# The recurrence's steps stand between the projections of its gate and of attention's queries and keys, which use two banks there in place of four

## The reference

```
z = xn @ w_in
qa = rmsnorm(qa.reshape(B, T, A_HEADS, HEAD_DIM), q_gain)
ka = rmsnorm(ka.reshape(B, T, A_HEADS, HEAD_DIM), k_gain)
...
attn = einsum('bnthk,bnshk->bnhts', q_dec, k_in) * mask
o_intra = einsum('bnhts,bnshv->bnthv', attn, v)
u = einsum('bnshk,bnshv->bnhkv', k_out, v)
def step(s, inp):
    d, uu = inp
    return d[..., None] * s + uu, s
...
o = o_intra + o_inter            # o_inter from q_dec and the state before the block
ob = rmsnorm(ob, out_gain) * silu(gb)
z = concatenate([oa, ob]); out = z @ w_out
```

## Time and profile before

| | us |
|---|---|
| median of 3 runs (1215.68 to 1221.85) | 1216.68 |
| the profiled execution, its own time | 1219.2 |
| its span in the profile | 1217.5 |
| end of the last projection unit | 227.0 |
| first score maximum of attention | 276.4 |
| mean granted clock of TensorE | 0.921 |

### The profile page before, as it was taken

The page is one execution under the profiler, slowest core; times in us unless marked ns, Lnnn a source line. Parts: engine busy times, 40 slices in busy tenths (PEclk is TensorE's granted clock), DMA queues, the critical chain, the costliest instruction groups (busy, mean ns, idle before and its releaser), DMA issues.

```text
span 1217.5 us, 20227 instructions
## 1 busy us (share of the span) xinstructions
PE 1027.6 (84%) x8691; PEld 802.2 (66%) x8691; DVE 435.5 (36%) x935; ACT 282.5 (23%) x543; POOL 181.0 (15%) x146
## 2 busy tenths in 40 slices
PE   5998999777999899977777299999998999778771
PEld 4988999654599755543444199999997555444440
DVE  5324584357734711100110574565446111011104
ACT  4244322115721211211111422222211112111110
POOL 4344331002000012111111000000000122111010
PEclk9999999856989999988888689999999999898886
DMA  6322321401084779999998713323578699999956
GB/s 215 84 78 72 102 83 38 112 11 53 13 306 178 279 271 418 416 417 416 416 415 309 233 52 88 105 80 129 208 128 348 257 416 416 416 417 416 416 239 229
DMA packets 114862, 282.83 MB, mean 232 GB/s; under 512 B 22954, under 2 KB 70102, under 8 KB 98356
## 3 DMA queue, kind: packets, MB, share of 16 engines
q1 hardware_dynamic: 105044, 263.66, 58.5%
q0 software_dynamic: 9728, 17.85, 4.0%
HBM read 270.57 MB, written 27.02 MB: 244 GB/s over the span
## 4 chain that ended last, share of the span: by engine, by line
PE 57%; DMA 24%; DVE 9%; SPq 4%; ACT 2%; issue 2%; POOL 1%; DVEq 0%; POOLq 0%; ACTq 0%
DMA w<-in_w_dram 19%; PE banks L1010 12%; PE banks L938 11%; PE banks L660 8%; PE banks L878 8%; PE banks L949 4%; PE banks L659 3%; SPq L389 3%; DMA wab<-in_w_in_ab_dram 2%; DVE XF L1289 2%; DMA yab<-y_rows 1%; POOL wab_lo L563 1%; PE banks L837 1%; PE banks L821 1%; PE banks L635 1%
## 5 line engine op out<-in xcount | busy, mean ns | idle before, releaser
L938 PE MATMUL banks<-w,xgT 128*64 128x256 f32 x2048 | 258.4, 412 | 73.4 <-DMA w<-in_w_dram 72.3
L938 PEld LDWEIGHTS banks<-w,xgT 128*64 128x64 f32 x2048 | 161.0, 149 | 179.2 <-DMA w<-in_w_dram 75.6
L1655 DVE TENSOR_TENSOR hh<-banks,sg 128x128 f32<-128x128 f32 x64 | 18.7, 292 | 412.6 <-ACT sg L1220 412.6
L575 POOL DMA_INDIRECT y_rows<-ys,yidx x64 | 63.7, 995 | 386.9 <-ACT ys L1228 385.6
L949 PE MATMUL banks<-w,hT 128*64 128x512 f32 x512 | 116.9, 598 | 0.0
L1010 PE MATMUL banks<-xc_hi,wc_hi 128*128 128x272 f32 x384 | 111.8, 291 | 2.1 <-DVE xc_lo L1302 2.1
L1010 PE MATMUL banks<-xc_hi,wc_lo 128*128 128x272 f32 x384 | 112.3, 292 | 0.0
L1010 PE MATMUL banks<-xc_lo,wc_hi 128*128 128x272 f32 x384 | 111.5, 290 | 0.0
L571 POOL DMA_INDIRECT xr<-x_rows,gidx x32 | 33.5, 1045 | 417.5 <-DVE yidx L1640 399.3
L660 PE MATMUL banks<-wab_hi,xc_hi 128*128 128x256 f32 (+1 forms) x320 | 91.4, 286 | 0.7 <-POOL wab_lo L563 0.7
L660 PE MATMUL banks<-wab_hi,xp_lo 128*128 128x256 f32 (+1 forms) x320 | 90.4, 283 | 0.0
(11 more groups left out here) (284 smaller groups left out, 1803.7 us busy)
## 6 DMA issues: line engine op xcount, KB each, us to landing
w<-in_w_dram SPq DMA_DIRECT2D x192, 1024.0 KB, 22.8
wab<-in_w_in_ab_dram SPq DMA_DIRECT2D x13, 1024.0 KB, 5.1
wc<-in_w_in_c_dram SPq DMA_DIRECT2D x24, 512.0 KB, 6.2
yab<-y_rows SPq DMA_DIRECT2D x16, 512.0 KB, 7.0
wo<-in_w_out_ab_dram SPq DMA_DIRECT2D x4, 1024.0 KB, 5.4
x_rows<-XF SPq DMA_DIRECT2D x8, 512.0 KB, 9.6
wo<-in_w_out_c_dram SPq DMA_DIRECT2D x4, 1024.0 KB, 5.6
H<-in_x_prompt_dram SPq DMA_DIRECT2D x4, 512.0 KB, 8.3
```

The source lines that it names most:

```text
L575: pool.indirect_dma_start(y_dram[l][:, :], bass.IndirectOffsetOnAxis(ap=index.bitcast(U32), axis=0), ys[i][:, :], None, bounds_check=4 * T ...
L938: last = pe.matmul(bank[hb][64 * f:64 * f + 64, 0:2 * P].rearrange("p (w j) -> p w j", w=2), xgT[i][:, k, 64 * ab:64 * ab + 64], w13[s][:, ...
```

## The change

Units 26 to 48 (output gate, queries, the first half of the keys) now alternate between banks 0 and 1 alone, so a unit waits for the one two earlier. Banks 2 to 7 go to the recurrence, whose steps stand between these units: keys and products of chunk c after unit 27+c, the updates of chunk 0 after unit 32, then for each chunk a pattern of three units: output of c and updates of c+1 behind unit 34+3c, `hgrn_T` of c behind unit 36+3c. DVE's chain of states is cut in halves, one each behind the reading of units 34+3c and 35+3c. Unit 49, the first on four banks again, waits for the whole recurrence (`st_ok` and `zB_ok` at 5). The values' units keep only `rows_T`, and attention follows the last of them. Several tiles move in SBUF (states, `kr`, `am`, `zB`); no arithmetic changes.

```
+SHARED = range(FIRST[6], FIRST[11])
+UNIT_BANK = [u % 2 if u in SHARED else u % 4 for u in range(UNIT_END[-1])]
...
-            return len([u for u in range(unit + 1) if u % 4 == b])
+            return len([u for u in range(unit + 1) if UNIT_BANK[u] == b])
...
             def unit(n, a):
                 u_ = FIRST[n] + a
+                b = UNIT_BANK[u_]
                 if u_ >= 4:
-                    pe.wait_ge(z_free[u_ % 4], u_ // 4)
+                    pe.wait_ge(z_free[b], freed(u_, b) - 1)
+                if u_ == SHARED.stop:
+                    pe.wait_ge(st_ok, NC)
+                    pe.wait_ge(zB_ok, NC)
...
             def hgrn_T(c):
                 n = ROWS[c]
                 pe.wait_ge(zt_ok, c + 1)
-                pe.wait_ge(a_ok, NC)
-                if c >= 2:
-                    pe.wait_ge(zB_ok, c - 1)
+                pe.wait_ge(st_ok, min(c + 2, NC))
...
             for n in range(1, 14):
                 pe.wait_ge(w_lo, n + 1)
                 for a in range(UNITS[n]):
                     unit(n, a)
+                    beside = FIRST[n] + a - SHARED.start
+                    if 1 <= beside <= NC:
+                        hgrn_keys(beside - 1)
+                        hgrn_products(beside - 1)
+                    if beside == 6:
+                        hgrn_updates(0)
+                    if 8 <= beside <= 20 and beside % 3 == 2:
+                        c = (beside - 8) // 3
+                        hgrn_out(c)
+                        if c + 1 < NC:
+                            hgrn_updates(c + 1)
+                    if 10 <= beside <= 22 and beside % 3 == 1:
+                        hgrn_T((beside - 10) // 3)
                     if n >= 12:
                         rows_T(NC * (n - 12) + a)
-                        i = NC * (n - 12) + a
-                        (hgrn_products if i % 2 else hgrn_keys)(i // 2)
-            hgrn_updates(0)
-            for c in range(NC):
-                if c + 1 < NC:
-                    hgrn_updates(c + 1)
-                if c > 0:
-                    hgrn_T(c - 1)
-                hgrn_out(c)
...
+            def hgrn_chain(c, half):
+                groups = range(ROWS[c] // PAIR)[2 * half:2 * half + 2]
...
                 dve.tensor_tensor(d, d, bc(gain[0:n, :].unsqueeze(1), four), ALU.mult).then_inc(qk_ok, 1)
+                c, step = divmod(i, 3)
+                if c < NC and step == 0:
+                    if c + 1 < NC:
+                        hgrn_chain(c + 1, 0)
+                    hgrn_sums(c)
+                if c < NC and step == 1:
+                    if c + 1 < NC:
+                        hgrn_chain(c + 1, 1)
+                    hgrn_norm(c)
+                if c < NC and step == 2:
+                    hgrn_gate(c)
...
-            hgrn_chain(0)
-            for c in range(NC):
-                if c + 1 < NC:
-                    hgrn_chain(c + 1)
-                hgrn_sums(c)
-                if c == NC - 1:
-                    hgrn_gate(c - 1)
-                hgrn_norm(c)
```

More of the change, by code:

```diff
@@ L699, in hgrn_keys @@
                     pe.wait_ge(hg_ok, 2)
-                else:
-                    pe.wait_ge(a_ok, c)
+                if c >= 2:
+                    pe.wait_ge(ko_ok, c - 1)
                 for m in range(4):
-                    last = pe.transpose(bank[4][0:ROWS[c], m * P:(m + 1) * P], kinT[:, m, c * P:c * P + ROWS[c]], ident[:])
+                    last = pe.transpose(bank[6 + c % 2][0:ROWS[c], m * P:(m + 1) * P], kinT[:, m, c * P:c * P + ROWS[c]], ident[:])
                 last.then_inc(ko_mm, 1)
             def hgrn_products(c):
-                pe.wait_ge(ko_ok, c + 1)
+                if c < 2:
+                    for b in range(2 + 2 * c, 4 + 2 * c):
+                        pe.wait_ge(z_free[b % 4], freed(SHARED.start - 1, b % 4))
+                else:
+                    pe.wait_ge(a_ok, c - 1)
                 for m in range(4):
@@ L717, in hgrn_updates @@
             def hgrn_updates(c):
-                pe.wait_ge(ko_ok, c + 1)
                 if c == 0:
-                    for b in range(4):
-                        pe.wait_ge(z_free[b], 16)
+                    pe.wait_ge(ko_ok, NC)
+                    pe.wait_ge(a_ok, NC)
                 else:
                     pe.wait_ge(st_ok, c)
+                if c >= 2:
+                    pe.wait_ge(zB_ok, c - 1)
                 for m in range(4):
@@ L797, in scores @@
                     pe.wait_ge(s_ok, 2 * j)
+                else:
+                    pe.wait_ge(qkT_ok, 2 * NC)
+                    for b in range(4):
+                        pe.wait_ge(z_free[b], freed(UNIT_END[-1] - 1, b))
                 if c == 4:
@@ L1093, in _, with hgrn_key_rows, hgrn_square, hgrn_root @@
             act.activation(lbe[:], lbe[:], ACT.Exp).then_inc(lbe_ok, 1)
+            def hgrn_key_rows(c):
+                n = ROWS[c]
+                act.wait_ge(ko_mm, c + 1)
+                act.activation(kr[c][0:n, :], bank[6 + c % 2][0:n, :], ACT.Copy).then_inc(ko_ok, 1)
+            def hgrn_square(c):
+                n = ROWS[c]
+                act.wait_ge(o_mm, c + 1)
+                if c > 0:
+                    act.wait_ge(hms_ok, c)
+                act.activation(osq[0:n, :].rearrange("p (q n) -> p q n", q=2), banks[0:n, 6:8, 0:256], ACT.Square).then_inc(osq_ok, 1)
+            def hgrn_root(c):
+                n = ROWS[c]
+                act.wait_ge(hms_ok, c + 1)
+                if c > 0:
+                    act.wait_ge(zt_ok, c)
+                act.activation(oms[0:n, :], oss[0:n, :], ACT.Sqrt, bias=epsc[0:n, 0:1], scale=1.0 / HD).then_inc(orms_ok, 1)
             for n in range(6):
@@ L1371, in _, with hgrn_mask @@
             dve.tensor_tensor(qdecT[:], qdecT[:], fT[:], ALU.mult).then_inc(hg_ok, 1)
-            for b in range(4):
+            def hgrn_mask(c):
+                n = ROWS[c]
+                dve.wait_ge(a_mm, c + 1)
+                for par in range(2):
+                    last = dve.copy_predicated(am[c][0:n, par, :, :],
+                                               bc(tri_mask[0:n, :].bitcast(U32).unsqueeze(1), [n, 4, PAIR]),
+                                               bank[2 + 2 * (c % 2) + par][0:n, 0:4 * PAIR].rearrange("p (m t) -> p m t", m=4))
+                last.then_inc(a_ok, 1)
@@ L1373, in _ @@
+            dve.wait_ge(hg_ok, 2)
+            for i in range(NC):
+                tie(dve.memset(am[i][:], 0.0))
+            dve.wait_ge(rb_dma, 32)
+            tie(dve.memset(st[0][:], 0.0))
+            for c in range(NC):
+                hgrn_mask(c)
+            hgrn_chain(0, 0)
+            hgrn_chain(0, 1)
+            for b in range(2):
                 dve.wait_ge(z_free[b], freed(UNIT_END[7] - 1, b))
```

175 lines of the change are left out of this document (78 added, 97 removed).

## The result

The changed kernel takes 1226.0 us (median of 13 runs), the kernel before 1219.0 on the same chip (13 runs): a ratio of 1.0055, with a 95% interval of 1.0035 to 1.0075. It is slower by 7 us. The profiled execution has a span of 1222.3 us, against 1217.5 before, 4.8 longer.

What follows compares the result with a forecast made beforehand. It took the recurrence alone to hold everything up behind the projections. Saving 37.0 us, adding 40.6 of work and waits and 4.5 of clock, less half a microsecond, gave +7.5 on 1216.7: 1224 us, range 1211 to 1233.

Steps and rivals of the forecast that it cites:

- What is saved behind the projections: From last unit to first score maximum: 49.4 us shrinks to 12.4, as bias copies still wait; 37.0 us saved.
- Outputs: The recurrence's output matmuls put between units on PE: 3.2 us a chunk, 3.0 for the small one, 15.8 in all.
- the ratio of 0.83: Updates at upper against lower clock level, 0.86 for 53 passes against 1.13 for 58; used to size outputs at 3.2 us.
- The rival that had the outputs scale with the clock: Clock never falls between units, outputs take 2.0 us: 1214, or 1207 if attention gains too; chance 0.20.
- Updates and transposes: New small PE work between the units: updates 4.0 us in all, transposes of ot 2.5 us in all.
- Waits for ot: PE at hgrn_T waits for DVE's late ot: 2.35 us four times, 0.5 for the small chunk, 9.9 in all.
- POOL's holds: Three POOL passes, with units 34, 39 and 44, hold DVE operations: about 0.8, 4.2 and 1.2 us, 6.2 in all.
- The state held: Chunk 2's last state operation on DVE caught behind POOL's second pass, 4.2 us late; rival that it isn't: 1220, chance 0.15.
- Unit 49's wait: Unit 49 waits for zB of the last chunk, behind unit 48's reading and the gate: about 2.2 us.
- Two banks aren't the wait: Between the units, DVE reads a query unit in 1.91 us plus a square, less than the 2.85 us unit between.
- The clock: Three or four falls of some 3.5 us on PE between the units, each slowing a dense unit: 4.5 us.
- that rival: PE's instructions come late beside DMA, at outputs and behind the projections: +1 to +4 us; counted within the forecast's 0.45.

Runs made afterwards that it cites:

- Experiments 4: The changed kernel with attention's bias copied in two halves by heads, eight copies in place of four; ratio 1.0011 to the kernel before.
- experiment 9: The changed kernel with the transposes of ot one unit later and GpSimd's wab_lo pass in four parts, bias in four copies; ratio 0.9880 to the kernel before.
- experiment 10: The kernel before with the bias copied in two halves and nothing else; ratio 0.9985 to the kernel before.
- experiment 2: The changed kernel with GpSimd's pass that makes wab_lo issued in four parts; ratio 0.9949 to the kernel before.
- Experiments 3 and 7: The kernel before with units 26 to 48 on two banks, ratio 1.0109; the same with GpSimd's wab_lo pass in four parts as well, 0.9947.

## Why the prediction held, step by step

- **What is saved behind the projections.** Predicted 37.0; measured 49.45 - 12.41 = 37.0. The rows that the forecast names add up to 12.2 behind the last unit (238.7 + 0.48 - 226.98), where it says 12.4. The copies took 10.3 us to the slowest landing (10.2 in the earlier trace rows), now bare. Experiments 4, 9 and 10 show it from both sides.
- **Outputs.** Predicted 3.2 us a chunk, measured 2.6; with 2.2 for the small one 12.6 in place of 15.8. The step that I mis-sized is the ratio of 0.83 from two rows of the chain, which list 53 and 58 passes. The second isn't of the lower level alone: the granted clock was 0.67 from 232.0 to 233.2 us. The whole group of 64 takes 0.91 at the upper level and 1.28 at the lower, 0.71, and the outputs 0.65. The rival that had the outputs scale with the clock came to 10.3 in all and was nearer on this term; the estimate of 3.2 by the Trainium skill (TensorE: Matmul & The Clock Gate, Single matmul latency) doesn't agree with the 2.6 either: that section is on one matmul's latency, and these follow each other closely.
- **Updates and transposes.** Predicted 4.0 and 2.5 us in all. The updates took 0.91 each at the upper level, 4.0 in all from their starts to those of the units behind; the transposes took 0.41 to 0.77 each in the same way, 2.4 in all.
- **Waits for ot.** Predicted 9.9 us of them and 6.2 through POOL's holds, 16.1; measured 15.0. One by one they were 2.63, 6.41, 2.43, 2.95 and 0.59. The undisturbed one of chunk 2, 2.43, is the 2.35 of the forecast. Chunk 0's first pass held DVE's tensor_scalar for 3.24 us, but got through with 0.3 where I had counted 0.8. Chunk 3's wait was put together wrongly: the small chunk behind it has one group of states and not two halves of two, so there is no chain ahead of its norm, and the forecast for it should have been 0.5, as for the small chunk itself (0.59). The other 2.4 are the third pass's hold, for which I had counted 1.2: the tensor_scalar took 2.57 in place of 0.17.

```profile
207.03 2.57 DVE L1479 TENSOR_SCALAR hms<-hss 128x4 f32<-128x4 f32 x1
```

With the pass in parts the wait is 1.03, of which 0.5 are two short holds. PE's transposes for chunk 3, in the changed kernel and with the pass in parts:

```profile
211.86 0.73 PE L781 MATMUL banks<-ident,ot 128*128 128x128 f32 x4 [2.95 <-DVE ot L1425]
```
```profile
200.45 0.66 PE L784 MATMUL banks<-ident,ot 128*128 128x128 f32 x4 [1.03 <-DVE ot L1428]
```

- **The state held.** I took the close case, the last state operation of chunk 2 caught for 4.2 us. It was caught, in the norm's way for chunk 1, for 4.47, 0.31 us after the pass began. The Trainium skill, SBUF — State Buffer, section Who interferes with whom, says that the later of the two blocks for the whole instruction, and the traces agree: 4.47 us behind one pass of 4.49, and 1.24 behind one part of 1.28 (experiment 2).
- **Unit 49's wait.** Predicted 2.2, measured 1.7.
- **Two banks.** "Two banks aren't the wait" stood for the changed kernel: no unit waited for z_free. As a general statement it was too bold. Experiments 3 and 7 show that two banks lay bare each hold of a reading, 13.4 us if nothing else stands in between. In the changed kernel PE was already late at these places, waiting for ot and putting out outputs, so the same holds cost it less.
- **The clock.** Predicted 4.5 us in three or four falls. Units 40, 43 and 46 lost 1.4, 1.7 and 1.6, together 4.7. Unit 26 lost 1.5 more, but that isn't the change's: the same unit, behind the same wait of 3.0, ran at the upper level in the kernel before and at the lower in experiment 10, whose code is the same up to there.
- **What I had left out.** Keys and products, which the forecast let change place for nothing, cost 0.8 more among the gate's units than among the values': the gaps behind units 27 to 31 grew by 5.8 us and the units among them by 0.1 each, and the gaps behind units 54 to 62 shrank by 5.6. And each break of the row of units loses the 0.16 us by which one unit starts before the last one ends, which over some eleven breaks is 1.8. PE's instructions came late by 0.7 us once (issue), less than the 1 to 4 of that rival.

The sum of what was measured: -37.0 + 12.6 + 4.0 + 2.4 + 15.0 + 1.7 + 0.7 (issue) + 0.8 + 6.2 + 1.8 = +8.2, within 0.1 of the table's 8.3. The forecast had 8.1 for the same stretch, out of terms that were off by up to 3.2 with opposite signs, and 3.3 us (issue, keys and products, breaks) that it didn't have; and 1.5 of the measured sum is unit 26's chance. That it came out so near is in part luck.

## What to carry to other kernels

Moving a serial stage into the gaps of a dense one wins only what the dense engine would otherwise idle; here PE kept every one of its small matmuls and got the hand-offs as waits on top. It came out ahead only when the transposes had a unit of cover and the pass was cut (experiment 9). Before taking buffers away from a stage, or putting a chain into it, look for the operations that another engine's long pass holds today without cost, and cut that pass first: this one edit was worth 0.6% in the kernel before, and 1.6% there with two banks (0.9947 against 1.0109). And a transfer that starts only when the stage ends comes out when its cover is moved, so split it by what is used first.

## What the runs showed of the chip

- A long pass of GpSimd costs VectorE in proportion to one instruction's length, not to the pass's: in four parts the pass takes 5.13 us in place of 4.49, and the operation behind it 1.24 in place of 4.47. VectorE gets in between two parts.
- Tiny matmuls (32 x 64) gained less from the clock than its factor of two: 0.65 us at the upper level for what takes 1.00 at the lower, and 0.91 for 1.28.
- Behind the same 3.0 us without a matmul, with the same code ahead of it, unit 26 took 4.6 to 4.8 us in five traces and 3.3 in two. Units 40, 43 and 46, behind waits of 2.4 to 6.4 us, took 4.4 to 4.6 in place of 2.9 to 3.0 in both traces of that code. Matmuls that nobody reads, put into that time, kept the granted clock at 1.00 up to 220 us, and another unit, behind a wait that had no fillers, fell in their stead.
- The copies of bias in halves shortened PE's time at the granted clock of 0.50 in attention by 10 us, from 30.7 to 20.5, although the first maximum came only 5.2 us earlier behind the last unit.
